# Hybrid attention and mixture-of-experts block: rotary by shifted copies, seven half-block products per gate chunk, b1 split later, ScalarE scaling in the second attention

## The reference

```python
h = rmsnorm(x, norm1_g)
qa, ka, va, qb, kb, vb, ga, gb = split(h @ w_in + b_in)       # 512 512 512 512 128 128 1024 1024
oa = neighborhood_attention(qa, ka, va, na_rpb)               # 8 heads of 64
ob = sliding_window_gqa(rope(qb), rope(kb), vb, swa_sinks)    # 8 query heads, 2 key heads
merged = sigmoid(ga) * (oa @ w_up_a) + sigmoid(gb) * (ob @ w_up_b)
x = x + merged @ w_out
x = x + moe_clamped_swiglu(rmsnorm(x, norm2_g), w_router, b_router, w1, b1, w2, b2)  # 4 of 32 experts
return rmsnorm(x, final_g)
# rope, per head of 64: concatenate([x1*cos - x2*sin, x2*cos + x1*sin]), x1, x2 the halves of 32
```

## Time and profile before

| | |
|---|---|
| median of 3 runs | 1129.65 us (1129.54 to 1130.3) |
| profiled execution, its time / its span | 1130.74 / 1128.8 us |
| PE / DVE / ACT / POOL busy | 1074.9 / 288.4 / 103.5 / 11.1 us |
| bytes over DMA | 436.35 MB, mean 387 GB/s |
| granted TensorE clock | 0.999 of full |

### The profile page before, as it was taken

The page is one execution under the profiler, slowest core; times in us unless marked ns, Lnnn a source line. Parts: engine busy times, 40 slices in busy tenths (PEclk is TensorE's granted clock), DMA queues, the critical chain, the costliest instruction groups (busy, mean ns, idle before and its releaser), DMA issues.

```text
span 1128.8 us, 12991 instructions
## 1 busy us (share of the span) xinstructions
PE 1074.9 (95%) x5165; PEld 477.1 (42%) x5165; DVE 288.4 (26%) x614; ACT 103.5 (9%) x220; POOL 11.1 (1%) x20
## 2 busy tenths in 40 slices
PE   8999999999999999999999999999999999999996
PEld 7888788733333333333333333333333333333332
DVE  4346422322222222222222222222211122222213
ACT  1130430200000000000000000000000000000001
POOL 1100000000000000000000000000000000000000
PEclk9999999999999999999999999999999999999999
DMA  9954258599999999999999999999999999999996
GB/s 358 420 216 154 78 214 380 205 347 411 427 427 429 428 429 428 429 427 428 428 430 428 429 427 429 427 429 428 430 429 428 428 428 427 429 429 428 430 423 259
DMA packets 35781, 436.35 MB, mean 387 GB/s; under 512 B 4432, under 2 KB 4944, under 8 KB 6992
## 3 DMA queue, kind: packets, MB, share of 16 engines
q1 hardware_dynamic: 34752, 435.10, 92.0%
q10 hardware_dynamic: 1008, 0.95, 0.3%
HBM read 434.98 MB, written 1.05 MB: 386 GB/s over the span
## 4 chain that ended last, share of the span: by engine, by line
PE 79%; DMA 13%; SPq 3%; DVE 3%; issue 1%; another core or an unknown queue 0%; ACT 0%; POOL 0%; POOLq 0%; DVEq 0%
PE bank L811 32%; PE bank L873 17%; DMA ring<-in_w 13%; PE bank L533 8%; PE bank L787 5%; PE bank L737 4%; PE bank L743 3%; SPq L354 3%; PE bank L647 2%; PE bank L629 2%; DVE work L1232 2%; PE bank L529 1%; PE bank L715 1%; PE bank L488 1%; PE bank L553 1%; PE bank L582 1%
## 5 line engine op out<-in xcount | busy, mean ns | idle before, releaser
L811 PE MATMUL bank<-ring,work 128*64 128x512 f32 x2048 | 450.8, 593 | 20.6 <-DMA ring<-in_w 20.0
L811 PEld LDWEIGHTS bank<-ring,work 128*64 128x64 f32 x2048 | 147.6, 137 | 303.2 <-issue 273.4
L873 PE MATMUL bank<-ring,work 128*64 128x512 f32 x1024 | 233.9, 599 | 17.6 <-DVE work L1232 17.5
L873 PEld LDWEIGHTS bank<-ring,work 128*64 128x64 f32 x1024 | 67.8, 136 | 141.4 <-issue 115.6
L1222 DVE TENSOR_SCALAR work<-bank 128x512 f32<-128x512 f32 x32 | 22.1, 692 | 387.5 <-PE bank L811 387.5
L533 PE MATMUL bank<-ring 128*128 128x256 f32 x432 | 96.5, 382 | 0.0
L533 PEld LDWEIGHTS bank<-ring 128*128 128x128 f32 x432 | 81.2, 190 | 13.1 <-issue 2.4
L1366 ACT ACTIVATE work<-work 128x512 f32<-128x512 f32 x32 | 20.1, 629 | 722.3 <-DVE work L1222 722.3
L787 PE MATMUL bank<-work 64*128 64x512 f32 x256 | 63.6, 615 | 1.3 <-DVE work L1202 1.3
L737 PE MATMUL bank<-x2n,work 128*64 128x512 f32 x256 | 61.9, 605 | 0.8 <-DVE work L1137 0.8
L1148 DVE TENSOR_TENSOR work<-bank,vec 128x256 f32<-128x256 f32 x64 | 24.2, 420 | 134.5 <-PE bank L743 134.5
(11 more groups left out here) (175 smaller groups left out, 446.1 us busy)
## 6 DMA issues: line engine op xcount, KB each, us to landing
ring<-in_w SPq DMA_DIRECT2D x184, 2048.0 KB, 40.7
ring<-in_w_in SPq DMA_DIRECT2D x16, 1024.0 KB, 24.4
ring<-in_w SPq DMA_DIRECT2D x15, 1024.0 KB, 10.1
ring<-in_w_out SPq DMA_DIRECT2D x4, 1024.0 KB, 4.7
ring<-in_w_up_a SPq DMA_DIRECT2D x2, 1024.0 KB, 10.1
ring<-in_w_up_b SPq DMA_DIRECT2D x2, 1024.0 KB, 7.2
ring<-in_na_rpb SPq DMA_DIRECT2D x1, 1536.0 KB, 19.1
ring<-in_w SPq DMA_DIRECT2D x2, 512.0 KB, 29.4
```

The costliest lines, as they stand in the source:

```text
L811: last = pe.matmul(bank[CAP * a:CAP * (a + 1), bk, :], kT, pairs[:, pair_of(par, k // 2), at + q * 512:at + (q + 1) * 512], start=False, s ...
L873: last = pe.matmul(bank[CAP * a:CAP * (a + 1), BH, :], fT, pairs[:, pair_of(par, c), at + a * 512:at + (a + 1) * 512], start=f == 0, stop= ...
```

## The change

1. **Rotary.** The permutation products and their constants go. ACT copies the four query blocks and the keys with each head's halves of 32 partitions exchanged (shift_blocks, during chunks 8 and 9), the sign sits in the sin table, and DVE combines them in SBUF during chunk 9; keys are duplicated by two DVE and two ACT copies.
2. **Seven products.** For gate chunks 11 to 16, weights and hT are cut into 2 by 2 blocks (halves of k, and of channels or tokens). Seven products of sums of blocks replace eight: 28 products 128 columns wide instead of 16 of 256 columns. POOL makes four weight sums per chunk in SBUF (128x512 each), DVE four sums of hT once, and DVE combines the seven results (mix_first, mix_second, eight operations of 128x128) into the gate blocks.
3. **Order.** PE makes the scores before it turns the probabilities, and turns them halfway through the chunk. ACT takes the exponentials before it copies the turned probabilities.
4. **Second attention.** ACT, not DVE, divides the exponentials by their sum (scale_probs) and copies the result out of PSUM. The sigmoids of all gates are taken after the chunks, in two parts.
5. **b1.** Its three loads are issued after the last probabilities are turned, and DVE splits it ahead of the merges. One expert load that uses the place waits for the split.

```diff
-_W_ATTN = [("rot", P), ("dup", 2 * P), ("dup_rot", 2 * P), ("cos", T), ("sin", T), ("na_mask", GRID_W),
+_W_ATTN = [("cos", T), ("sin", T), ("na_mask", GRID_W),
            ("swa_mask", MT * T)]
...
-        ROPE_C = GATE_C + 1
+        ROPE_C = GATE_C
+        SEVEN_C = GATE_C + 2
...
-                if n == 20:
-                    sp.wait_ge(probT_done, 4)
-                    for part in range(PARTS):
-                        sp.dma_start(b1_raw[part * E:(part + 1) * E, :], b1[0]).then_inc(b1_landed, 16)
...
+            sp.wait_ge(probT_done, UNITS)
+            for part in range(PARTS):
+                sp.dma_start(b1_raw[part * E:(part + 1) * E, :], b1[0]).then_inc(b1_landed, 16)
             sp.wait_ge(o_done, UNITS)
-            for c in range(1, 5):
+            for c in range(1, 4):
                 load_chunk(0, c, 0, up)
+            sp.wait_ge(b1_split, 1)
+            load_chunk(0, 4, 0, up)
             load_chunk(1, 2, 1, up + 2)
             load_chunk(1, 3, 1, outp)
...
+                n, s = c - SEVEN_C, w_sums[:, c % 2]
+                pool.wait_ge(landed[slot_of(c)], landings(c))
+                if n >= 2:
+                    pool.wait_ge(chunk_used, c - 1)
+                pool.tensor_tensor(s[:, 0], w_block(c, 0, 0), w_block(c, 0, 1), ALU.subtract).then_inc(w_sum_ready, 1)
+                pool.wait_ge(w_sum_ready, 4 * n + 1)
+                pool.tensor_tensor(w_block(c, 0, 1), w_block(c, 0, 1), w_block(c, 1, 1), ALU.add).then_inc(w_sum_ready, 1)
+                pool.wait_ge(w_sum_ready, 4 * n + 2)
+                pool.tensor_tensor(s[:, 1], w_block(c, 0, 1), w_block(c, 0, 0), ALU.subtract).then_inc(w_sum_ready, 1)
+                pool.wait_ge(w_sum_ready, 4 * n + 3)
+                pool.tensor_tensor(s[:, 2], w_block(c, 1, 0), s[:, 1], ALU.subtract).then_inc(w_sum_ready, 1)
+
+            pool.wait_ge(rope_ready, 2)
+            for c in range(SEVEN_C, N_IN):
+                weight_sums(c)
...
+            def product(dst, a, b):
+                for k in range(4):
+                    last = pe.matmul(dst, a[:, k, :], b[:, k, :], start=k == 0, stop=k == 3)
+                return last
+            def gate_products(c, part):
+                n, s = c - SEVEN_C, w_sums[:, c % 2]
+                phase = 2 * n + part
+                if phase == 0:
+                    pe.wait_ge(proj_read_dve, GATE_C)
+                elif phase < 3:
+                    pe.wait_ge(proj_read_act, phase)
+                else:
+                    pe.wait_ge(gate_part_read, phase - 2)
+                dst = quarter(gate_bank(c, part))
+                if part == 0:
+                    pe.wait_ge(landed[slot_of(c)], landings(c))
+                    product(dst[:, 0, :], w_block(c, 0, 0), h_block(0, 0))
+                    pe.wait_ge(w_sum_ready, 4 * n + 1)
+                    if n == 0:
+                        pe.wait_ge(h_sums_ready, 4)
+                    product(dst[:, 1, :], s[:, 0], h_sums[:, 2])
+                    pe.wait_ge(w_sum_ready, 4 * n + 2)
+                    product(dst[:, 2, :], w_block(c, 0, 1), h_sums[:, 0])
+                    pe.wait_ge(w_sum_ready, 4 * n + 3)
+                    product(dst[:, 3, :], s[:, 1], h_sums[:, 1]).then_inc(gate_half_done, 1)
+                else:
+                    product(dst[:, 0, :], w_block(c, 1, 0), h_block(1, 0))
+                    product(dst[:, 1, :], w_block(c, 1, 1), h_sums[:, 3])
+                    pe.wait_ge(w_sum_ready, 4 * n + 4)
+                    product(dst[:, 2, :], s[:, 2], h_block(1, 1)).then_inc(chunk_used, 1)
...
+                    if a and turned is not None:
+                        turn_probs(turned)
...
-                    pe.wait_ge(rope_ready, 1)
+                    pe.wait_ge(rope_ready, 2)
+                    pe.wait_ge(k_shifted, 2)
...
-            def rotate():
...
-                for b in range(4):
-                    pe.matmul(half_(BT + b // 2)[:, b % 2, :], C("rot"), qbT[:, b, :], start=True, stop=True)
-                for g in range(KV_HEADS):
-                    pe.matmul(half_(BO)[:, g, :], C("dup")[:, g * P:(g + 1) * P], kraw[:], start=True, stop=True)
-                    last = pe.matmul(half_(BK)[:, g, :], C("dup_rot")[:, g * P:(g + 1) * P], kraw[:],
-                                     start=True, stop=True)
-                last.then_inc(rope_done, 1)
...
-                if turned is not None:
-                    turn_probs(turned)
                 if scored is not None:
                     scores(scored)
-                if c:
-                    project(c)
+                if c >= SEVEN_C:
+                    gate_products(c, 0)
+                    if turned is not None:
+                        turn_probs(turned)
+                    gate_products(c, 1)
+                elif c:
+                    project(c, turned)
                 else:
                     project_first()
                 if turned is not None:
                     attend(turned)
-                if c == ROPE_C:
-                    rotate()
...
+            def sum_tokens():
+                dve.wait_ge(scores_done, 4)
+                dve.tensor_tensor(h_sums[:, 2], h_block(1, 1), h_block(0, 1), ALU.subtract).then_inc(h_sums_ready, 1)
+                dve.tensor_tensor(h_sums[:, 0], h_block(0, 1), h_block(0, 0), ALU.subtract).then_inc(h_sums_ready, 1)
+                dve.wait_ge(h_sums_ready, 2)
+                dve.tensor_tensor(h_sums[:, 1], h_block(1, 1), h_sums[:, 0], ALU.subtract).then_inc(h_sums_ready, 1)
+                dve.wait_ge(h_sums_ready, 3)
+                dve.tensor_tensor(h_sums[:, 3], h_sums[:, 1], h_block(1, 0), ALU.subtract).then_inc(h_sums_ready, 1)
...
+            def mix_first(c):
+                dve.wait_ge(gate_half_done, c - SEVEN_C + 1)
+                m1, m7, m5, m6 = (quarter(gate_bank(c, 0))[:, q, :] for q in range(4))
+                bias = [vec[:, 2 * c + a:2 * c + a + 1] for a in range(2)]
+                if c > SEVEN_C:
+                    dve.wait_ge(gate_part_read, 2 * (c - SEVEN_C))
+                ch.link(dve.tensor_copy(mixed[:, 0], m1))
+                ch.link(dve.tensor_tensor(mixed[:, 1], m6, mixed[:, 0], ALU.add))
+                dve.scalar_tensor_tensor(out=mixed[:, 2], in0=m5, scalar=bias[0], in1=mixed[:, 1], op0=ALU.add, op1=ALU.add)
+                ch.link(dve.scalar_tensor_tensor(out=mixed[:, 3], in0=m7, scalar=bias[1], in1=mixed[:, 1],
+                                                 op0=ALU.add, op1=ALU.add))
+                dve.tensor_tensor(gate_of(c, 1, 1), m5, mixed[:, 3], ALU.add).then_inc(gate_part_read, 1)
+            def mix_second(c):
+                dve.wait_ge(chunk_used, c + 1)
+                m2, m4, m3 = (quarter(gate_bank(c, 1))[:, q, :] for q in range(3))
+                dve.scalar_tensor_tensor(out=gate_of(c, 0, 0), in0=m2, scalar=vec[:, 2 * c:2 * c + 1], in1=mixed[:, 0],
+                                         op0=ALU.add, op1=ALU.add)
+                dve.tensor_tensor(gate_of(c, 1, 0), mixed[:, 3], m4, ALU.subtract)
+                dve.tensor_tensor(gate_of(c, 0, 1), m3, mixed[:, 2], ALU.add).then_inc(gate_part_read, 1)
...
+                cos, sin = (C(n).rearrange("p (o t) -> p o t", o=1).to_broadcast([P, 2, T]) for n in ("cos", "sin"))
+                for b in (0, 2):
+                    dve.wait_ge(shift_copied, b // 2 + 1)
+                    q, s = qbT[:, b:b + 2, :], shifted[:, b:b + 2, :]
+                    dve.tensor_tensor(s, s, sin, ALU.mult)
+                    ch.link(dve.tensor_tensor(q, q, cos, ALU.mult))
+                    ch.link(dve.tensor_tensor(q, q, s, ALU.add))
+                s = shifted[:, 4, :]
+                dve.wait_ge(shift_copied, 3)
+                dve.tensor_tensor(s, s, C("sin"), ALU.mult)
+                ch.link(dve.tensor_tensor(kraw[:], kraw[:], C("cos"), ALU.mult))
+                dve.tensor_tensor(kraw[:], kraw[:], s, ALU.add).then_inc(k_turned, 1)
+                dve.wait_ge(k_turned, 1)
+                for g in range(KV_HEADS):
+                    rows = slice(DH * g, DH * g + DH)
+                    dve.tensor_copy(kbT[rows, g, :], kraw[rows, :]).then_inc(rope_ready, 1)
...
+                if u >= 4:
+                    dve.reciprocal(den[:], den[:]).then_inc(den_ready, 1)
+                    return
...
+                if c > SEVEN_C:
+                    mix_second(c - 1)
+                if unit_at(TURN_C, c - 1) is not None and c - 1 <= GATE_C:
                     read_output(unit_at(TURN_C, c - 1))
+                if c == GATE_C:
+                    rotary()
+                    sum_tokens()
                 if scored is not None:
                     softmax_front(scored)
+                if c >= SEVEN_C:
+                    mix_first(c)
                 if scored is not None:
                     softmax_back(scored)
...
+            mix_second(N_IN - 1)
+            dve.wait_ge(b1_landed, 16 * PARTS)
...
+            def scale_probs(u):
```

(49 more changed lines are left out.)

90 lines of the change are left out of this document (33 added, 57 removed).

## The result

The changed kernel takes 1123.82 us, median of six executions (1122.62 to 1125.35), beside 1129.91 (1129.54 to 1132.66) for the kernel before: a ratio of 0.9941, 95% interval 0.9931 to 0.9952. The profiled execution took 1124.16, with a span of 1122.0. A second, unchanged build gave 1123.05 beside 1130.57, 0.9935 (0.9921 to 0.9948). So the change is faster by 6 to 7.5 us; the forecast was 1122.2 and a gain of 7.5. One execution of the last variant ("Both together") ran at a mean granted clock of 0.761 and took 1454.28 us; its median and ratio leave it out.

A forecast was written before the change was run, and what follows sets the result against it. PE ahead of the up stage was taken to bound the kernel by setting when the saturated expert-weight stream starts. Savings of 3.46 + 5.1 = 8.6 us, less a 1.1 us stall, gave 7.5 us: median 1122.2, range 1120.6 to 1127.2.

The forecast's parts named there:

- Permutation products: On PE, from 98.58 us to the start of chunk 11 at 102.04: removing them saves 3.46 us.
- Seven products: Gate chunks 11 to 16 on PE: 6.25 us instead of 7.10 each, 0.85 less per chunk, 5.1 us for six.
- A narrow product costs no more per column here: Gate chunks on PE: 128-column products at 0.223 us each, against 0.222 us for 128 columns of the wide ones.
- the 0.23 that the prediction named as a sign of being wrong: Gate chunks on PE: narrow products above 0.23 us each would show the forecast wrong.
- only their order changes: Scores, turning and values on PE: cost as before, 1.06, 1.03 and 1.01 us, so no gain.
- The softmax loop: Second attention: VectorE's small instructions wait for GpSimd, stalling PE before unit 4's values by 1.1 us (0 to 3.5).
- GpSimd's sums: Weight sums for gate chunks: 1.33 us each, starting near 91.4, chunk 11 ready near 97, PE wait taken as 0.
- b1: Up stage: landing 7 to 12 us in, split ending at 17 to 21.5, cover until 22.8; cost 0 (0 to 3).
- The saturated stream moves ahead by as much: Expert-weight loads: PE time saved before the up stage at 156.8 us moves the whole stream ahead equally.

The follow-up runs named there:

- Both together: Changed kernel with chunk 10 also in seven products and, in the second attention alone, ScalarE's copy of turned probabilities before the exponentials: 1121.26 us, 0.992 of before.
- the run with eight products: Changed kernel with gate chunks 11 to 16 computed as before (16 products of 256 columns, no sums), rest of the change kept: 1125.92 us, 0.9964 of before.
- copies first: Changed kernel with ScalarE copying the turned probabilities ahead of the exponentials in each chunk: 1122.54 us, 0.9933 of the kernel before.
- the first experiment: The changed kernel built again with no edit, to narrow the ratio: 1123.05 us, 0.9935 of the kernel before.
- seven from chunk 10: Changed kernel with chunk 10 in seven products too, GpSimd's sums and the sums of hT starting earlier: 1123.21 us, 0.9926 of the kernel before.

## Why the prediction came out

It was right on the mechanism: PE time saved ahead of the up stage reached the end. At the up stage the size was 7.46 against 7.5, but this closeness is luck. Three terms were off and cancelled: the seven products by 1.2 us too much, the order by 0.8 us too little, the stall by 0.4 us too much. The median, 1123.82, is 1.6 us above the forecast.

- **Permutation products, 3.46 us.** Right, by 4.23 - 0.77.
- **Seven products, 5.1 us.** The mis-sized term. By U it is 3.9: the whole 7.46, less 3.46, less 0.77, plus the stall of 0.7; the run with eight products less the one with copies first gives 3.95. I took 3.57 us for 16 narrow products from the chain, whose pieces are cut elsewhere than the rows of PE: there the time from the start of L537 (77.78) to the next start (81.45) is 3.67, 0.229 each. And I set it beside the 7.10 us that the chain gives chunk 10; by its starts in the rows (91.41 to 98.42) that chunk took 7.01. So each side was off by 0.1 us, and the gain of a chunk is 0.65 and not 0.85. Behind scores both forms cost 0.1 more, 7.11 and 6.45, and the difference stays. Chunk 13 of before, behind scores; its next start is 126.38:
```profile
119.27 7.17 PE L533 MATMUL bank<-ring 128*128 128x256 f32 x32
```
"A narrow product costs no more per column here" was wrong. 56 products of 128 columns take 12.70 us, 0.227 each; 32 products of 256 columns take 14.01, 0.219 for 128 columns, so narrow ones cost 3.7% more. Behind scores a narrow one comes to 0.230, just at the 0.23 that the prediction named as a sign of being wrong.
- **Turning: "only their order changes".** Wrong by 0.77 us of gain, which the prediction had put at nothing.
- **The softmax loop, 1.1 us.** Right in its place (the values of unit 4) and in the contention; 0.7 in size. From the scores' start S = 111.83 the copy was due at S+9.4 and came at S+9.1; PE was ready at S+8.45 (forecast 8.34). One link had another cause than forecast. VectorE began unit 5's maximum 1.1 us late, about the 1.0 forecast, which the prediction put down to the mixing of chunk 12 and the end of unit 4's softmax as such. In the run without weight sums both stand there too, and VectorE is on time, 1.2 us behind the start of the scores. It was late because unit 4's own small instructions had waited for GpSimd. The wait at the maximum itself was 0.63 us (0.79 against 0.16), forecast 1.0. The other units lost nothing visible, as forecast, though small instructions waited there too (0.85 in chunk 15). The Trainium skill ("SBUF — State Buffer", Who interferes with whom) says that a VectorE instruction with two SBUF inputs contends with a GpSimd instruction that reads SBUF. The prediction had no tensor_tensor row for it, and now 0.69 against 1.75 us, and 0.16 against 1.21, bear it out.
- **GpSimd's sums.** 1.27 us each (forecast 1.33), at a distance of 1.35; 1.59 to 1.77 while they alternate with VectorE's. PE never waits for them in the changed kernel. The rows of the changed kernel:
```profile
91.38 1.77 POOL L489 TENSOR_TENSOR ring<-ring 128x512 f32<-128x512 f32 x1 [58.65 <-DVE ring L1087]
...
96.57 1.60 POOL L495 TENSOR_TENSOR ring<-ring 128x512 f32<-128x512 f32 x1
...
104.54 1.27 POOL L489 TENSOR_TENSOR ring<-ring 128x512 f32<-128x512 f32 x1 [1.11 <-PE bank L539]
```
The start at 91.4 was right to a tenth; chunk 11 is ready at 98.2 instead of 97, since alternation costs both engines. PE reaches the chunk at 97.97 (forecast 98.6, though the sum given for it, 82.5 + 2 x 7.1 + 2.04, is 98.7). By 0.907 us a product it wants hT's sums, ready at 97.04, near 98.9, and GpSimd's fourth near 103.4, so the 0 for this term held, with 1.8 us left on the nearer of the two.
- **b1.** Right. It lands 11.0 us into the up stage and its split ends at 20.6 (forecast 7 to 12 and 17 to 21.5); no wait of PE. The landing took 9.5 us against 5.7. No run takes the late b1 or ScalarE's scaling away alone; at the up stage the terms above make up the whole 7.46 without them. The changed kernel:
```profile
160.12 1.22 DVE L1155 CAST b_parts<-ring 96x2048 bf16<-96x2048 f32 x1 [11.19 <-DMA ring<-in_b]
...
168.50 1.22 DVE L1160 CAST b_parts<-ring 32x2048 bf16<-32x2048 f32 x1
...
178.28 1.22 DVE L1184 TENSOR_TENSOR ring<-ring 128x1024 f32<-128x1024 f32 x1
```
- **From the up stage to the end.** "The saturated stream moves ahead by as much" held, 7.46 to 7.65 us at the experts' first product (224.97 before, 217.32 after). The totals scatter behind that for two reasons. From there to the span's end it is 903.1 to 905.1 us in all thirteen profiled executions, 903.83 before and 904.68 after; what sets that scatter stays open. It also hides whether b1's new place costs the stream anything, the rival of the first experiment: with the old place it is 903.1 and 903.8, with the new one 903.3 to 905.1. And from the up stage to the first product it is 68.21 to 68.23 in nine of them. Two of the others waited for b1's split (69.65 and 72.85, above); the last two, 70.74 in the unchanged build and 70.75 in seven from chunk 10, are those where the clock fell in the router. The same stretch of the unchanged build, then of the changed kernel:
```profile
207.50:212.50 5.00, 4.90 (x37) 3.42 (x29) 2.30 (x14) 1.18 (x3) 0.71 (x1) 0.72 0.99 362
212.50:217.50 5.00, 3.56 (x10) 0.78 (x9) 2.49 (x14) 2.29 (x4) 0.00 (x0) 0.60 0.59 166
```
```profile
207.50:212.50 5.00, 4.82 (x46) 3.70 (x44) 2.72 (x15) 1.25 (x3) 0.71 (x1) 1.00 0.78 265
212.50:217.50 5.00, 2.91 (x16) 1.16 (x18) 3.21 (x17) 3.95 (x6) 0.00 (x0) 1.00 0.80 262
```
The same code is 2.5 us apart. PE's waits there differ by 0.02 us, and its rows take longer (one of 12 records 2.20 us from start to start against 1.51), so this is the clock. So a profiled total of one execution carries 2.5 us of this and 2 of the stream, more than most edits here.

## What to carry to other kernels

Take a price per instruction from start to start of neighbours in steady state, not from a piece of the chain: 0.1 us on each of two rows was a quarter of a term here. Before giving GpSimd two-input work, list what VectorE does between SBUF and SBUF at that time, however small, and see what hangs on it; then let ScalarE do first what the bottleneck asks for first. Measure a change ahead of a saturated stream at the point where it ends, here the up stage: U repeated within 0.03 us where totals of one kernel differed by 3 to 4. Of a wait on the bottleneck, count also what the clock does behind it.

## What the runs showed of the hardware

- TensorE at a granted clock of 1.00 (2.4 GHz): 128 columns of a 128x128 f32 product cost 0.219 us at 256 columns each and 0.227 at 128; turning (eight records of 128x128) costs 0.87 us between two halves of a chunk, 1.03 between value products and scores, and 0.93 between value products and a chunk.
- With GpSimd adding, even a 128x4 instruction of VectorE takes up to 1.21 us against 0.16, and GpSimd itself slows from 1.27 to 1.77 us when the two alternate.
- The same program does not always get the same clock: through the router it stayed at 1.00 in eleven of the thirteen profiled executions and fell to 0.50 (210 to 215 us) in two, one of them the unchanged build.
- Behind waits of PE the granted clock fell to 0.78 after 2.70 us, to 0.62 after 4.38 and to 0.52 after 6.09. After 3.00 us it fell in one execution (0.66) and stayed at 1.00 in another; after waits of 0.66, 1.19 and 1.53 it stayed at 1.00.
